# Two transformer blocks on one core: the router between mixer and experts shortened, the recurrence's gate arithmetic issued in pieces

## The reference

```python
# mixer: a recurrence with a forget gate, beside a stick-breaking attention
log_f = logaddexp(log(lb), log1p(-lb) + log_sigmoid(zf))   # lb is 0 in layer 0
k_in  = (1 - lb) * sigmoid(-zf)
o_a = rms_norm(hgrn2_chunkwise(silu(hq), k_in, hi, log_f)) * silu(hog)
o_b = stick_breaking_attention(sq, sk, sv)
y = sigmoid(ga) * (o_a @ w_branch_a) + sigmoid(gb) * (o_b @ w_branch_b)
x = x + y @ w_out
# experts, layer 1
logits = t @ w_router                                      # 256 x 8
top_val, top_idx = top_k(logits, 2)
combine = softmax(top_val) scattered to 256 x 8
y = sum over 8 experts of combine[:, e] * swiglu(t, w_gate[e], w_up[e], w_down[e])
```

## Time and profile before

| | us |
|---|---|
| median of 3 runs | 2535.65 (2533.25 to 2537.75) |
| the profiled execution, its own time | 2533.39 |
| its span, first to last instruction | 2531.6 |
| busy in the span | PE 2389.5 (94%), DVE 1799.5 (71%), ACT 1373.5 (54%), POOL 31.6 (1%) |
| mean granted clock of TensorE | 0.979 |
| the experts, stretch 870 to 1890 of the span | PE busy 1013.96 of 1020 |
| the second block, from 1890 on | 642 of the span |

### The profile page before, as it was taken

How to read it: one execution, slowest core, us unless ns; L and a number is a source line. 1 busy time by engine, 2 the same in 40 slices (tenths; PEclk the granted TensorE clock), 3 DMA queues, 4 the chain that set the end, 5 groups by cost and what they waited for, 6 DMA issues and landing times. The chain is left out here.

```text
span 2531.6 us, 34886 instructions
## 1 busy us (share of the span) xinstructions
PE 2389.5 (94%) x13745; PEld 2028.5 (80%) x13745; DVE 1799.5 (71%) x1710; ACT 1373.5 (54%) x1357; POOL 31.6 (1%) x25
## 2 busy tenths in 40 slices
PE   6898999997998699999999999999998999989998
PEld 6898899997898588888888888888865875568967
DVE  5764655556764588888888888888877656746684
ACT  5463555446463376777676767676752220434362
POOL 0100000000100000000000000000000000000000
PEclk9999999998999799999999999999999999999999
DMA  6234466662334198989898989898960220025300
GB/s 246 84 134 150 176 243 245 243 225 106 111 134 167 67 365 340 364 340 364 339 363 343 362 336 367 331 374 329 376 256 34 83 100 1 1 71 106 107 1 18
DMA packets 81646, 531.70 MB, mean 210 GB/s; under 512 B 16919, under 2 KB 17080, under 8 KB 17336
## 3 DMA queue, kind: packets, MB, share of 16 engines
q1 hardware_dynamic: 80560, 525.21, 56.0%
q10 hardware_dynamic: 968, 4.78, 0.5%
HBM read 528.90 MB, written 1.05 MB: 209 GB/s over the span
## 5 line engine op out<-in xcount | busy, mean ns | idle before, releaser
L2188 DVE TENSOR_TENSOR ring_low<-ring,M_high 128x2048 fp32r<-128x2048 f32 x336 | 760.7, 2290 | 123.7 <-ACT M_high L1228 112.1
L1228 ACT ACTIVATE M_high<-ring 128x2048 fp32r<-128x2048 f32 x336 | 631.2, 1909 | 2.6 <-DMA ring<-panels 2.4
L423 PE MATMUL ps<-M_high,xe_parts 128*128 128x512 f32 x1792 | 599.4, 397 | 2.4 <-DVE xe_parts L2199 2.4
L423 PEld LDWEIGHTS ps<-M_high,xe_parts 128*128 128x128 f32 x1792 | 336.5, 188 | 70.2 <-DVE xe_parts L2199 2.6
L423 PE MATMUL ps<-ring_low,xe_parts 128*128 128x512 f32 x896 | 349.8, 390 | 0.0
L2060 DVE TENSOR_TENSOR W_low<-ring,W_high 128x2048 fp32r<-128x2048 f32 x66 | 150.0, 2291 | 101.7 <-ACT W_high L1228 101.7
L423 PE MATMUL ps<-h_parts,B_high 128*128 128x256 f32 x1024 | 194.6, 292 | 20.5 <-DVE ring_low L1856 12.7
L1228 ACT ACTIVATE arena<-ps 128x256 f32<-128x256 f32 (+3 forms) x243 | 116.0, 477 | 177.4 <-PE ps L423 148.1
L423 PE MATMUL ps<-h_parts,ring_low 128*128 128x256 f32 x704 | 204.1, 290 | 0.0
L423 PEld LDWEIGHTS ps<-ring_low,xe_parts 128*128 128x128 f32 x896 | 168.7, 188 | 32.3
L423 PEld LDWEIGHTS ps<-h_parts,B_high 128*128 128x128 f32 x1024 | 166.0, 199 | 22.5 <-DVE ring_low L1856 13.3
(11 more groups left out here) (270 smaller groups left out, 4445.4 us busy)
## 6 DMA issues: line engine op xcount, KB each, us to landing
ring<-panels SPq DMA_DIRECT2D x496, 1024.0 KB, 4.8
arena<-rpb SPq DMA_DIRECT2D x32, 64.0 KB, 8.1
cst<-consts SPq DMA_DIRECT2D x1, 1760.5 KB, 8.9
xT<-x SPq DMA_DIRECT2D x1, 1024.0 KB, 4.8
cT<-ctx ACTq DMA_DIRECT2D x1, 1024.0 KB, 7.7
arena<-dft ACTq DMA_DIRECT2D x1, 1024.0 KB, 9.0
y<-xT ACTq DMA_DIRECT2D x1, 1024.0 KB, 3.9
proj<-w ACTq DMA_DIRECT2D x1, 512.0 KB, 6.0
```

The lines of the kernel that those rows point to most:

```text
L423: return nc.tensor.matmul(o, w, m, start=start, stop=stop, skip_group_check=skip)
L1228: return nc.scalar.activation(o, i, fn, **kw)
L2188: V.tensor_tensor(wide_low(q, 0, PW), ring[:, (q % RING) * PW:(q % RING + 1) * PW], moe_high(q, 0, PW).bitcast(F32), ALU.subtract).then_in ...
```

## The change

Three places are edited. Nothing in the second block is (its Hyena and attention code has no line in the diff, but for the POOL program, whose work there now follows one new step).

1. **Gates in pieces.** `prelude` is cut in three on DVE (`forget_abs` at i = 1, `forget` at i = 2, `decay_sums` at i = 2 in layer 0 and at i = 4 in layer 1) and on ACT (`forget_log` at i = 1; then `hgrn_key` at i = 2 in layer 0, or `bounded_log` at i = 3 in layer 1). Layer 1's second exponential works in a buffer of its own, `e1`. SHIFT becomes (1, 3), so all interleaved work of layer 1 comes one panel later.
2. **`mix_out`** waits only for the first piece of y before its first panel, and for the others before the second.
3. **The router.** The ranking takes both halves of the tokens in one instruction each; three products count the places; the diagonals and `combine` move into `every_expert`; SEL comes first, SELW is made by POOL; PE gathers the first expert's tokens before the branch; ACT makes the high parts of the first two expert panels before it exponentiates the logits.

```diff
-        SHIFT = (1, 2)
+        SHIFT = (1, 3)
 # PE, mix_out
-                pe.wait_ge(sem("y_parts_ready"), nth(pe, "y_parts_ready", 3))
+                pe.wait_ge(sem("y_parts_ready"), 3 * layer + 1)
...
                         q = take_split()
+                        if j == 0 and br == 1:
+                            pe.wait_ge(sem("y_parts_ready"), nth(pe, "y_parts_ready", 3))
 # PE, router
-                for tb in range(2):
-                    for k in range(KD):
-                        if tb == 0:
-                            pe.wait_ge(sem("h_ready"), nth(pe, "h_ready"))
-                        last = mm(bank(1)[:, tb * 8:tb * 8 + 8], h3[:, k, tb * P:(tb + 1) * P],
+                for k in range(KD):
+                    pe.wait_ge(sem("h_ready"), nth(pe, "h_ready"))
+                    for tb in range(2):
+                        last = mm(bank(tb)[:, 0:8], h3[:, k, tb * P:(tb + 1) * P],
...
-                for j in range(4):
+                for j in (2, 3, 0, 1):
...
-                mm(o[:, 0:8], K(K_STRICT), s0, True, True)
-                mm(o[:, 8:16], K(K_ONE), s0, True, False)
-                mm(o[:, 8:16], K(K_STRICT), s1, False, True)
-                mm(o[:, 16:24], K(K_ONE), s0, True, False)
-                mm(o[:, 16:24], K(K_ONE), s1, False, True).then_inc(sem("places_ready"), 1)
-                pe.wait_ge(sem("combine_diagonals_ready"), nth(pe, "combine_diagonals_ready"))
+                mm(o[:, 0:16], K(K_STRICT), both, True, False, True)
+                mm(o[:, 8:24], K(K_ONE), both, False, False, True)
+                mm(o[:, 16:24], K(K_ONE), rt[:, 40:48], False, True, True).then_inc(sem("places_ready"), 1)
+                pe.wait_ge(sem("h_tokens_copied"), nth(pe, "h_tokens_copied"))
+                pe.wait_ge(sem("selection_ready"), nth(pe, "selection_ready"))
+                gather_tokens(0)
+                pe.wait_ge(sem("weighted_selection_ready"), nth(pe, "weighted_selection_ready"))
+                for j in range(16):
+                    last = nc.tensor.transpose(bank(2 + j // 4)[:, (j % 4) * P:(j % 4 + 1) * P],
+                                               SELW[:, j * P:(j + 1) * P], K(K_ID))
+                last.then_inc(sem("slot_weights_ready"), 1)
+                pe.wait_ge(sem("crowded_ready"), nth(pe, "crowded_ready"))
...
-                pe.wait_ge(sem("slot_weights_copied"), nth(pe, "slot_weights_copied"))
-                pe.wait_ge(sem("h_tokens_copied"), nth(pe, "h_tokens_copied"))
 # PE, compact_experts, step
+                    if ex == 0 and f == 1:
+                        pe.wait_ge(sem("slot_weights_copied"), 1)
...
-                gather(0)
 # ACT, project1 and hgrn
-                    if i == 2:
-                        prelude()
+                    if i == 1:
+                        forget_log()
+                    elif i == 2 and layer == 0:
+                        hgrn_key()
+                    elif i == 3 and layer == 1:
+                        bounded_log()
...
+                def bounded_log():
+                    act.wait_ge(sem("forget_abs_ready"), nth(act, "forget_abs_ready"))
+                    f(e1, e1, ACT.Exp).then_inc(sem("bounded_exp_ready"), 1)
+                    hgrn_key()
+                    act.wait_ge(sem("bounded_exp_ready"), 1)
+                    f(e1, e1, ACT.Ln, bias=ones1).then_inc(sem("forget_log_ready"), 1)
 # ACT, compact_experts and before the router's exponentials
-                high(0)
                 tokens_high(0)
-                high(1)
+                act.wait_ge(sem("slot_weights_ready"), nth(act, "slot_weights_ready"))
+                f(G[:, S:S + 2048], bank(2, 4), ACT.Copy).then_inc(sem("slot_weights_copied"), 1)
...
+                    moe_panel_high(panel[0])
+                    moe_panel_high(panel[0] + 1)
                     act.wait_ge(sem("router_max_ready"), nth(act, "router_max_ready"))
 # POOL, after the levels of both layers
+            pool.wait_ge(sem("selection_ready"), nth(pool, "selection_ready"))
+            for tb in range(2):
+                ins = pool.tensor_tensor(SELW.rearrange("p (e t n) -> p e t n", e=8, t=2)[:, :, tb, :],
+                                         SEL.rearrange("p (e t n) -> p e t n", e=8, t=2)[:, :, tb, :],
+                                         rt[:, 200 + 8 * tb:208 + 8 * tb].unsqueeze(2).to_broadcast([P, 8, P]),
+                                         ALU.mult)
+            ins.then_inc(sem("weighted_selection_ready"), 1)
 # DVE, project1
                 for i in range(IN1):
+                    if i == 1:
+                        dve.wait_ge(sem("proj_copied"), IN1 * layer + 2)
+                        forget_abs()
                     if i < IN1 - 3:
                         proj_part(p0, i + 3)
...
                     if i == 2:
-                        dve.wait_ge(sem("proj_copied"), IN1 * layer + 2)
-                        prelude()
+                        forget()
+                    if i == 2 + 2 * layer:
+                        decay_sums()
 # DVE, forget, layer 1
+                    step(V.tensor_tensor(e0, lf, z, ALU.subtract))
+                    less = lbs[:, 0:4].unsqueeze(2).to_broadcast([P, 4, S])
+                    step(V.tensor_tensor(heads(lf), heads(lf), less, ALU.subtract))
+                    signal(V.scalar_tensor_tensor(e1, lf, -1.0, lf, ALU.mult, ALU.min), "forget_abs_ready")
+                    rest = lbs[:, 12:16].unsqueeze(2).to_broadcast([P, 4, S])
+                    signal(V.tensor_tensor(heads(e0), heads(e0), rest, ALU.add), "key_exponent_ready")
 # DVE, router, after places_ready
-            step(V.tensor_copy(rt[:, 216:240], bank(7)[:, 0:24]))
...
+            step(V.tensor_reduce(rt[:, 240:241], bank(7)[:, 16:24], AX.X, ALU.max))
             signal(V.tensor_scalar(crowded[0:1, 0:1], rt[0:1, 240:241], float(SLOTS), None, ALU.is_gt),
                    "crowded_ready")
+            step(V.scalar_tensor_tensor(place, bank(7)[:, 0:16], 1.0, sel, ALU.add, ALU.mult))
+            step(V.tensor_scalar(place, place, -1.0, None, ALU.add))
             for tb in range(2):
                 step(V.tensor_tensor(sel4[:, :, tb, :], K(K_IOTA).unsqueeze(1).to_broadcast([P, 8, P]),
                                      place[:, 8 * tb:8 * tb + 8].unsqueeze(2).to_broadcast([P, 8, P]), ALU.is_equal))
-                step(V.tensor_tensor(selw4[:, :, tb, :], sel4[:, :, tb, :],
-                                     rt[:, 200 + 8 * tb:208 + 8 * tb].unsqueeze(2).to_broadcast([P, 8, P]), ALU.mult))
-            announce("weighted_selection_ready")
-            dve.wait_ge(sem("slot_weights_ready"), nth(dve, "slot_weights_ready"))
-            announce("accumulators_free")
+            announce("selection_ready")
```

More of the change, by code:

```diff
@@ L704, in steps @@
                     down(p0 + 40, 0, er, e * FSTEP + (FSTEP - 1))
+                combine()
                 up(p0, 0, 0)
@@ L843, in gather @@
                         pe.wait_ge(sem("rows_added"), 4 * (ex - 1))
[L844 to L850 removed]
+                    gather_tokens(ex)
                 def up(ex, s, first, i):
@@ L1859, in project1 @@
             def project1(layer):
-                prelude, level, merged, hgrn_normed = hgrn(layer)
+                forget_abs, forget, decay_sums, level, merged, hgrn_normed = hgrn(layer)
                 stick_softplus, stick_weights, y_low = stick()
@@ L2140, in _ @@
-            signal(V.tensor_scalar(rt[:, 40:56], rt[:, 40:56], 1.5, None, ALU.is_lt), "selected_ready")
+            other = L3.unsqueeze(2).to_broadcast([P, 2, 8, 8])
+            own = L3.unsqueeze(3).to_broadcast([P, 2, 8, 8])
+            more = rt[:, 64:192].rearrange("p (t a b) -> p t a b", t=2, a=8)
+            tie = rt[:, 256:384].rearrange("p (t a b) -> p t a b", t=2, a=8)
+            low = K(K_LOW, 64).rearrange("p (a b) -> p a b", a=8).unsqueeze(1).to_broadcast([P, 2, 8, 8])
+            step(V.tensor_tensor(more, other, own, ALU.is_gt))
@@ L2141, in _ @@
+            step(V.tensor_tensor(tie, other, own, ALU.is_equal))
+            step(V.tensor_tensor(tie, tie, low, ALU.mult))
+            step(V.tensor_tensor(more, more, tie, ALU.add))
+            step(V.tensor_reduce(rt[:, 40:56], rt[:, 64:192].rearrange("p (a b) -> p a b", a=16), AX.X, ALU.add))
+            sel = rt[:, 40:56]
+            signal(V.tensor_scalar(sel, sel, 1.5, None, ALU.is_lt), "selected_ready")
             dve.wait_ge(sem("router_exp_ready"), nth(dve, "router_exp_ready"))
-            step(V.tensor_tensor(rt[:, 16:32], rt[:, 16:32], rt[:, 40:56], ALU.mult))
+            step(V.tensor_tensor(rt[:, 16:32], rt[:, 16:32], sel, ALU.mult))
```

119 lines of the change are left out of this document (48 added, 71 removed).

## The result

The changed kernel takes **2505.89 us** (median of 4 runs, 2501.86 to 2514.63), beside 2534.45 for the kernel before in the same measurement (2532.81 to 2537.75): a ratio of 0.989, with a 95% interval of 0.9859 to 0.9922, so 20 to 36 us less. The forecast was 2513.0 with a range of 2503 to 2522.

What follows compares the result with a forecast made beforehand. PE bounds the kernel: its experts' work stays, while the router's chain of small steps and the mixers' idle gaps can shrink. 2533.39 less 22.7 (17.5 + 3.0 + 2.2), plus 2.26, gives 2513 us; range 2503 to 2522.

Steps and rivals of the forecast that it cites:

- Router, 17.5: First expert product's effective start moves from 869.88 to 852.4, a gain of 17.5 us, with ends of 14 and 21.
- I keep it whole, behind the transposes: Router's branch on PE: loading the flag and jumping costs its full 4.5 us after the transposes, until 850.5.
- rival (b): Router's branch hides under the transposes and experts start warm: 21 from router, 5 and 2.5 from gates, 2507; chance 0.15.
- SELW on POOL: Router: POOL's two products at 2.355 us each run beside PE's gather, until 843.3, and are hidden by it.
- I expect DVE to ask later: Router: DVE's low part of panel 0 won't slip between POOL's two products; otherwise SELW would be 2.3 us late.
- rival (c): Router: POOL and DVE collide over SELW, costing 2.3 us and cold transposes; 14 from the router, 2516.5; chance 0.1.
- Gates in layer 1, 3.0: Layer 1's mixer: the gap ahead of panel 6 goes, smaller gaps come later; gain 3.0 us, ends 0 and 6.
- Gates in layer 0, 2.2: Layer 0's mixer: work up to level 0 comes 2.2 us earlier, gap 2.90 shrinks to 0.7; between 0 and 2.9.
- The 2.26 from the profiled run to the median: Whole kernel before: the median of three runs, 2535.65, lies 2.26 us above the profiled 2533.39; added at the end.
- Rival (a): Mixers: gates only move their gaps, PE idling 3.8, 2.5 and 2.5 with cold restarts; gates give about 0, 2518; chance 0.2.
- (d): Router: POOL's product with the broadcast weight is far dearer, so the whole is slower; 2547 at 20 us each; chance 0.02.
- (e): Early gather or SELW on POOL is blocked by a misread wait; only the gates' 5 us remain, 2531; chance 0.03.

Runs made afterwards that it cites:

- the second measurement: The changed kernel itself, unedited, measured again later beside the kernel before: 2509.87 us, ratio 0.9903.
- e1: The kernel before with the router edits alone, ACT's early panels among them; gates, SHIFT and `mix_out` as before: 2514.39 us, ratio 0.9915.
- e3: The changed kernel with SHIFT back at (1, 2): 2508.84 us, ratio 0.99.
- e4: The changed kernel; in layer 1 DVE builds the last unit's weights between the two panels of i = 20, not behind both: 2504.02 us, ratio 0.9881.
- e7: The changed kernel with `mix_out` waiting for all three pieces of y again: 2509.70 us (one run).
- e5: The changed kernel with the first expert's gather put back behind the branch: 2512.44 us (one run).
- e9: The changed kernel with products of zeros added on PE in layer 1, the router and the second attention, where it waits: 2504.21 us, ratio 0.9873.
- e6: The changed kernel with SELW's two products made by DVE behind the selection, not by POOL: 2509.07 us (one run).

## Why the prediction was right, and where it wasn't

The sign, the range and the split held: 22.7 were expected, 20 to 36 measured, 25.9 in the second measurement. By its own steps:

- **Router, 17.5.** Measured between landmarks: 21.2 up to the first expert product, less 1.4 for the experts' colder start, 19.8; over the six profiles with this router code (the changed kernel's two, e1, e3, e4, e7) it is 18.2 to 20.4. e1's median says 21.6, with an interval of 18 to 25. In the first profile the miss of 2.3 is the sum of four terms, and only the first of them is much the same in the other profiles.
  - *"I keep it whole, behind the transposes"* is the step that failed: the branch shows 2.83, not 4.5. The price was right, 4.43 to 4.80 from the start of the transposes (e5, and the changed kernel), but the transposes were already in PE's queue and cover their 1.97. That is rival (b)'s mechanism, without its warm start. 1.7 us.
  - The logits took 0.9 less in this execution (5.86 to the turning of the tokens; before 6.79, from 823.94 to 830.73); other profiles with the new logits code have 5.8 to 6.9, so this is chance and no gain of the edit.
  - The cold start of the experts cost 1.4, not 1.9: 0.5. This too is chance: in e7 the same code started warm and lost nothing, in e1 it lost 2.6.
  - The gather ended 14.0 behind the start of the turning, not 13.2: 0.8 the other way. The selection came 0.3 later, and the gather, cold behind its 3.59, took 5.71.
- **SELW on POOL.** 2 x 2.355 was right for neither: 1.90 for the product alone, 3.95 beside DVE. *"I expect DVE to ask later"* failed: DVE's branch took 1.29, not 4.5, so rival (c) did happen. That it cost nothing in the profiled execution was luck: the gather was slow enough to hide it. It cost 0.57 and 0.46 in e1 and e4, and with a fast gather it costs 1.98 (e9).
- **Gates in layer 1, 3.0.** The two profiled executions give 2.0, the like pairs 2.3 and 3.2. The walk itself came to 4.8 less 2.5, that is 2.3, and the 3.0 was taken above it without a reason. Its last step was right: counted from layer 1's first panel PE starts panel 8 where the walk had it, within 0.2 us (631.88, in a layer that starts 2.4 earlier than before; 634.5 was expected). The gap ahead of panel 6 went, and the idle time of 3.8 + 2.5 came as 6.40 in one piece ahead of level(0). Level(-1), said to wait 3.8, waited for nothing: the scans ended at 619.4, just before PE reached it at 620.09, and it ran ahead of level 0's exponent (623.82), by which the 3.8 were set. The signal that it waits for is given behind the scans, and DVE's two panels that stand ahead of it in the code (619.41 to 623.9) did not hold it back. The 2.5 ahead of `stick_out(1)` were 2.53. The colder clock cost 1.7 at level(0) alone.
- **`mix_out`.** The wait was worth 2.2 (e7), as the prediction needed it. What the whole got of it by the logits was 0.8, since behind its next gap, which the kernel before has too, PE was at a lower clock than in e7.
- **Gates in layer 0, 2.2.** The gap was right, 0.57 where 0.7 was expected: 2.3. But the term was put too low, since the like pairs give 4.4 and 4.0 (2.8 between the two profiled executions, which start their second panel differently). It left out the clock, which the layer 1 walk did reckon: with the first gap gone PE stayed at the upper clock behind the second, and level(0) took 2.05 in place of 3.46. The term's low end is 0 in the prediction's text and 1 in its sum; nothing hangs on it.
- **The 2.26 from the profiled run to the median.** This is the weak step of the whole comparison. Executions of one kernel here spread by 5 to 17 us, and stretches without any edit by 1 to 7; the changed kernel's profiled execution was 5 us above the median of its eight. A forecast against one profiled execution carries that spread, and the range's allowance of 2 was too little for it. That the first median fell inside the range owes something to this spread; the median of all eight runs, 2509.4, is 3.6 under the forecast, of which the branch's 1.7 and layer 0's 2 have a cause that the runs show.

Rival (a), that the gates only move their gaps, is half true: of layer 1's 11.32 + 1.9, 8.9 came back as gaps, and only the rest was gained. Rivals (d) and (e) are out: POOL's product takes 1.90, and all but the shift by a panel does what it says.

## What to carry to other kernels

Before pricing a branch or a load of a flag, look at what its engine has queued ahead of it: only what outlasts that work costs time, so put the decision behind a batch of products, and load the flag before a wait that is there anyway. When the longest gap of a stage is taken out, walk on with the old durations to the next wait: here 8.9 of 11.3 us stood there again, and the cheap repair was to change the order on the helping engine (e4), not to shift the whole pipeline (e3). For edits of a few microseconds in a kernel with many gaps, compare landmark to landmark over several profiles, and take the size of the spread from a second profile of the same code.

## What the runs showed of the chip

- A gap costs twice, and the second part isn't fixed. Behind the same gap of 2.3 us the same products took 8.79 or 10.18, at 1.00 or 0.83 of the clock; behind 4.87 us one execution was back at the upper clock after 8 us, another after 13. In layer 0 a gap of 2.63 that followed one of 2.90 left the next 16 products at 3.46; with the first of the two down to 0.57 they took 2.05. The mean clock was 0.977 to 0.984 over the changed kernel's eight runs, 0.984 to 0.987 with the gap of layer 1 filled with products of zeros.
- Idle time filled with products that compute nothing is worth having where PE has work right behind it: 1.7 us at level(0) for 5.13 us of zeros that hid in a gap of 6.40. Where another engine is late (the router) it is worth nothing.
- The same branch shows as 1.29 on DVE, 4.5 on PE with nothing queued ahead, 2.83 behind 1.97 of products, and 0.78 behind 3.65; loading the flag is about 0.9 of PE's.
- DVE and POOL lengthen each other: 2.89 for DVE's product of two operands that takes 2.29 alone (e6), and 3.95 for POOL's that takes 1.90. The Trainium skill's page "SBUF — State Buffer" (SBUF: two separate sides) has DVE and GpSimd share a pair of ports that is locked for a whole instruction. The trace agrees within 0.2 us: DVE, asking at 836.17, would then wait for POOL's first product (835.02 + 1.90 = 836.92) and run its 2.29 until 839.21, and it ended at 839.06; POOL's second would follow until 840.96, and it ended at 840.82. So the long rows hold a wait each, and the two engines took turns, which the prediction, with DVE behind both products, did not have.
